# Combining the expert outputs: the first addition of odd tiles as a scaling on ScalarE and an addition on GpSimd

## The reference

```python
gates = g_w * e_w / jnp.sum(e_w, axis=-1, keepdims=True)
yb = lax.map(expert_block, (xb, blk_exp)).reshape(n_slots, d)
y = jax.ops.segment_sum(yb.astype(f32) * slot_gate[:, None], slot_tok, num_segments=n + 1)
# per token: h + g1 * y_rows[slot 1] + g2 * y_rows[slot 2]
out = h * rsqrt(mean(h * h) + NORM_EPS) * norm_final_g
```

## Time and profile before

| | |
|---|---|
| three runs, us | 3441.44, 3448.67 (median), 3459.29 |
| profiled execution, us | 3445.74 |
| its span, first to last instruction, us | 3444.0 |
| busy over the span | PE 92%, DVE 38%, ACT 29%, POOL 10% |
| `combine`, from its first instruction at 3365.75 | some 78 us of the span |

### The profile page before, as it was taken

How to read it: one execution, slowest core, us unless ns; L and a number is a source line. 1 busy time by engine, 2 the same in 40 slices (tenths; PEclk the granted TensorE clock), 3 DMA queues, 4 the chain that set the end, 5 groups by cost and what they waited for, 6 DMA issues and landing times. The chain is left out here.

```text
span 3444.0 us, 75176 instructions
## 1 busy us (share of the span) xinstructions
PE 3163.8 (92%) x31053; PEld 2164.0 (63%) x31054; DVE 1315.9 (38%) x3229; ACT 1014.8 (29%) x2151; POOL 332.8 (10%) x348
## 2 busy tenths in 40 slices
PE   6999999999979988987999979996999999999990
PEld 4677666776758888876877655554555555555550
DVE  3455344553224433434755446664111111111117
ACT  3344433444222222224644453331111111111112
POOL 0000000000010000001433200001101010100104
PEclk9999999999879999998999989997999999999995
DMA  6111111111362342324766555423777786677658
GB/s 209 63 68 66 53 46 63 68 58 45 84 143 105 129 156 107 118 108 141 228 184 177 135 191 184 154 80 135 275 249 274 247 281 216 236 273 249 225 192 306
DMA packets 299222, 544.44 MB, mean 158 GB/s; under 512 B 98338, under 2 KB 122658, under 8 KB 292308
## 3 DMA queue, kind: packets, MB, share of 16 engines
q1 hardware_dynamic: 253052, 401.29, 35.1%
q10 hardware_dynamic: 25128, 66.26, 6.1%
q0 software_dynamic: 20784, 73.15, 5.8%
HBM read 400.66 MB, written 139.98 MB: 157 GB/s over the span
## 5 line engine op out<-in xcount | busy, mean ns | idle before, releaser
L298 PE MATMUL proj_main_ps<-proj_xt,proj_w 128*128 128x257 f32 (+1 forms) x1728 | 390.1, 381 | 0.0
L298 PEld LDWEIGHTS proj_main_ps<-proj_xt,proj_w 128*128 128x128 f32 x1728 | 327.8, 203 | 41.3
L2517 PE MATMUL moe_y_ps<-moe_w,moe_ht 128*64 128x512 f32 x1312 | 302.5, 603 | 3.1 <-ACT moe_ht L2556 3.1
L321 PE MATMUL proj_main_ps<-proj_w,proj_xt 128*128 128x512 f32 (+1 forms) x560 | 248.6, 597 | 0.0
L2265 PE MATMUL out_proj_ps<-out_w,out_ct 128*128 128x512 f32 x544 | 242.3, 599 | 5.7 <-DMA out_w<-in_w_out_dram 5.7
L2567 ACT ACTIVATE moe_sg<-moe_gate 128x256 f32<-128x256 f32 x82 | 31.5, 384 | 535.6 <-PE moe_gate L2501 535.6
L2517 PEld LDWEIGHTS moe_y_ps<-moe_w,moe_ht 128*64 128x64 f32 x1312 | 87.5, 137 | 159.5 <-issue 156.1
L321 PEld LDWEIGHTS proj_main_ps<-proj_w,proj_xt 128*128 128x128 f32 (+1 forms) x560 | 102.9, 185 | 124.4 <-issue 122.8
L1163 DVE COPY_PREDICATED rwkv_t<-ahead_rwkv_cons,rwkv_level_ps 128x512 f32<-128x512 uint32 (+1 forms) x168 | 109.2, 661 | 181.8 <-PE rwkv_level_ps L881 181.6
L2265 PEld LDWEIGHTS out_proj_ps<-out_w,out_ct 128*128 128x128 f32 x544 | 101.8, 192 | 121.9 <-issue 121.9
L2603 DVE COPY moe_y<-moe_y_ps 128x512 f32<-128x512 f32 x82 | 56.7, 692 | 314.9 <-PE moe_y_ps L2517 314.9
(11 more groups left out here) (351 smaller groups left out, 5521.2 us busy)
## 6 DMA issues: line engine op xcount, KB each, us to landing
moe_w<-in_expert_w_dram SPq DMA_DIRECT2D x64, 2048.0 KB, 9.7
y_rows<-rwkv_zero POOLq DMA_DIRECT2D x65, 512.0 KB, 4.8
kept_first_gate<-in_expert_w_dram SPq DMA_DIRECT2D x16, 2048.0 KB, 9.7
kept_first_up<-in_expert_w_dram SPq DMA_DIRECT2D x16, 2048.0 KB, 15.1
y_rows<-moe_y ACTq DMA_DIRECT2D x164, 128.0 KB, 6.1
ft_p<-proj_uf SPq DMA_DIRECT2D x32, 642.0 KB, 3.3
rwkv_feat<-ft_p SPq DMA_DIRECT2D x12, 1284.0 KB, 7.1
att_s_k<-in_cache_att_k_dram ACTq DMA_DIRECT2D x14, 1024.0 KB, 7.3
```

The lines of the kernel that those rows point to most:

```text
L298: last = mm(out[:, 0:w + 1], W[:, k, kind * C + m * P:kind * C + (m + 1) * P], XT[n % 2][:, k, 0:w + 1], start=(k == 0), stop=(k == KT - 1))
L321: last = mm(o, x, W[:, k, j * C:(j + 1) * C], start=(k == 0), stop=(k == KT - 1))
L2517: last = mm(py[j * HB:(j + 1) * HB, :], HT[:, c, r * HB:(r + 1) * HB], W2[s][:, k, j * 512:(j + 1) * 512], start=(k == 0), stop=(k == FE / ...
```

## The change

For odd tiles `add_first` is split in two. ACT multiplies Y1 by the gate in place (`weigh_first`), placed one tile ahead: before its Square of tile t it scales tile t+1 if that is odd. POOL adds the scaled Y1 to HH (`add_weighted`), placed four tiles behind its gathers: before the gathers of tile t it adds tile t-4 if that is odd, and its loop runs four steps further to reach the last ones. DVE's `add_second` of an odd tile waits for POOL's addition; DVE no longer issues `add_first` for odd tiles. Even tiles are computed as before. There are 8 odd tiles (1 to 15).

```diff
+        weighted, added = sem("first_weighted"), sem("weighted_added")
+        apart = lambda t: t % 2 == 1
 ...
         @blk.gpsimd
         def _(g):
-            for t in range(NT):
+            def add_weighted(t):
+                j, R = t % NB, rows(t)
+                g.wait_ge(weighted, t // 2 + 1)
+                nc.gpsimd.tensor_tensor(HH[0:R, t, :], HH[0:R, t, :], Y1[j][0:R], ALU.add).then_inc(added, 1)
+
+            for t in range(NT + 4):
+                if t >= 4 and apart(t - 4):
+                    add_weighted(t - 4)
+                if t >= NT:
+                    continue
                 j, R = t % NB, rows(t)
                 if t >= NB:
                     g.wait_ge(st[j], 16 * (t // NB))
 ...
             def add_second(t):
                 j, R = t % NB, rows(t)
-                v.wait_ge(first, t + 1)
+                if apart(t):
+                    v.wait_ge(added, t // 2 + 1)
+                else:
+                    v.wait_ge(first, t // 2 + 1)
 ...
             for t in range(NT + 1):
-                if t < NT:
+                if t < NT and not apart(t):
                     add_first(t)
 ...
         @blk.scalar
         def _(a):
+            def weigh_first(t):
+                j, R = t % NB, rows(t)
+                a.wait_ge(gat[j], 32 * (t // NB) + 32)
+                nc.scalar.activation(Y1[j][0:R], Y1[j][0:R], ACT.Identity, scale=RG[0:R, t, 0:1]).then_inc(weighted, 1)
+
             for t in range(NT):
                 j, R, n = t % NB, rows(t), N1[t % 2]
+                if t + 1 < NT and apart(t + 1):
+                    weigh_first(t + 1)
                 a.wait_ge(second, t + 1)
```

## The result

The changed kernel takes 3470.51 us (median of nine runs, 3467.45 to 3475.42) against 3442.39 us of the kernel before (nine runs, 3432.79 to 3463.47): 28.1 us more, ratio 1.0076 with a 95% interval of 1.0057 to 1.0096. The prediction said 3476, with 28.8 us of difference. The difference was met within a microsecond; most of the 5.5 us by which the time itself was missed come from the base, since the median of the kernel before is 3442.39 over nine runs, where it was 3448.67 over the first three. The profiled executions have spans of 3472.7 and 3444.0 us.

What follows compares the result with a forecast made beforehand. In `combine`, DVE and the DMA engines were taken as both full; six turns (+23.6), the start (+4.7) and the tail (+0.5) gave +28.8 us, so 3474.5 from the profile, predicted 3476 between two bases, range 3462 to 3490.

Steps and rivals of the forecast that it cites:

- the ring: In `combine`, store(u-1) waits on the add of u, queued behind gathers that wait for store(u-3); 11.9 us per two tiles.
- Store until POOL goes on: In `combine`, from issue of an output store until POOL can issue the gathers waiting for it: 4.2 us.
- Two gather issues: On POOL, two issues of 0.95 us with 0.30 behind each, ahead of the add: 2.5 us.
- Second addition to the end of the normalisation: On DVE, from the start of an odd tile's second addition to the end of the previous tile's normalisation: 2.7 us.
- The turn: Two tiles of `combine`: 4.2 + 2.5 + 2.5 + 2.7 = 11.9 us, where two now take 7.8 (7.97 over tiles 0 to 12).
- The start: Before store 0, the add of tile 1 stands behind ten gather issues on POOL: store 0 moves by +4.7 us.
- The tail: After store 12, the add of tile 15 overlaps the normalisation of tile 13 and may lose up to 1.2; +0.5 us.
- ACT's part: Eight scalings of 128x1024 on ACT, 1.1 us each, covered by its idle time; waiting for the next tile's gathers costs nothing.
- rival A: Not slower: POOL issues gathers in time and the add waits only for ACT's scaling, 7.9 us per two tiles; about 3450; 0.04.
- Rival B: Only shared SBUF reading: each add stops DVE for 2.4 us and saves it 1.2, +9.6 us, 3455; chance 0.06.
- Rival C: DMA engines stay full and the store wait stays 6.1 us: 13.8 a turn, +40.2 us, 3486; chance 0.15.
- Rival D: ACT loads a table for the scaling and again for the root, 2.6 us per odd tile; about +5, 3480; chance 0.05.

Runs made afterwards that it cites:

- the short addition: Changed kernel with POOL's addition covering only the first 64 of 1024 columns of an odd tile, the rest left out: stage 98.9 us, against 106.8 changed and 78.3 before.

## Why the prediction was right

By its terms, with what the trace of the changed kernel has:

- The order on POOL. The add of odd tile u stood behind the gathers of u+3 and the store of u-3, in six turns, as read from the code and the wait of the earlier trace rows. The edits that move the add three tiles behind or take more buffers remove 14.2 and 18.5 us without touching an operation, and the short addition leaves 20.6 us of loss with hardly any arithmetic: that is what shows the ring and rules out the length of the operations as its cause.
- Store until POOL goes on: 4.2 forecast; 4.15 to 4.71 until landing and 0.26 until the issue, so 4.4 to 5.0. Too low by some 0.5. That it came so near is in part luck: its reckoning counted only the gathers right behind the addition, and the run with the short addition, where these stand as before, has a landing of 5.4 to 5.7.
- Two gather issues: 2.5 forecast, 2.2 measured. The 0.30 us behind the second don't arise when an addition follows (3402.09 + 0.93, the addition at 3403.04). The two errors nearly cancel, by luck.
- The addition: 2.4 against 2.35, with handoffs 2.5 against 2.4 (3403.04 to 3405.43). Second addition to the end of the normalisation: 2.7 against 2.7 (3405.43 to 3408.11).
- The turn: 11.9 against 11.9; six of them +23.6 against +23.6.
- The start: +4.7 forecast. Store 0 goes 18.5 us after the gain's load, 14.4 before: +4.1. The 0.30 us behind the last gather issue don't arise here either.
- The tail: +0.5 forecast, +0.8 measured (16.8 us behind store 12 against 16.0), with the 3.41 us operation named in advance as the place of the overlap: 2.1 us lost there less 1.2 us saved is 0.9, within the 1.2 that were named as the most.
- Sum: +28.8 against +28.5 in the profile and +28.1 between the medians.

What was not right: ACT's part was priced at nothing. In the changed kernel that holds, but the run with the addition on DVE shows that it costs some 3.5 us with the ring gone (81.8 against 78.3, one profile of each). DVE's idle time ahead of the odd tiles' second additions was put at 4 to 5 us and is 5.0 to 5.6; the forecast's own terms (a turn of 11.9 less some 6.6 us of DVE's work) give 5.3. And rival A, the side on which the change would not have been slower, was put at 3450 by the scaling's chain; the run with eight buffers shows that POOL's own 8.8 us per two tiles, which I did not reckon, would have stood ahead of it. Rival B named the size of that case (+9.6 against +10.0) by luck: 4.2 of the 10.0 are the later start, and most of the rest is borne by POOL. Rival C (a store wait of 6.1) was the right thing to fear: with the short addition the wait reached 5.9, and 6.8 in the first turn. Rival D fell: the stage has one load of tables, as before.

No version was found that beats the kernel before. The stage with the ring and nearly all of POOL's arithmetic taken away, which doesn't compute the whole result, took 77.5 us against 78.3: a difference too small to be measured in 3442.

## What to carry to other kernels

An engine with idle time isn't an engine that is free at the time needed: look at what it waits for in its own order, and put on it only what may be as late as that wait. If an operation that others need is queued behind gathers that wait for stores of its own results, you get a ring; count its turn term by term, and remember that the transfer in it is no constant: here it grew when the addition ahead of it was shortened. Before taking work off the busiest engine, look for the second full resource: here, with the DMA engines at 1.03 and 420 GB/s, the ring gave back 2.4 of some 7 us of DVE work that it no longer had.

## What the runs showed of the hardware

- DVE operations with two SBUF inputs stand still while POOL adds or copies in SBUF: 128x1024 went from 1.28 us to 3.24 to 3.42 us beside an addition of 2.34 to 2.76, and to 1.86 to 2.53 us beside a one-input copy of 1.04 to 1.35. Each ended 1.07 to 1.09 us behind POOL's operation. Memsets on POOL (0.97 us) held up none.
- It goes the other way too. An indirect gather takes 0.94 us to issue in a quiet stretch; each of the 83 issues of more than 1.15 us began while a DVE operation was under way and ended 0.74 to 0.85 us behind it, after up to 2.00 us. No addition is needed for it: the kernel before has 1.84 us. POOL's addition of 2.35 us took 2.56 to 2.84 us where DVE was at work as it began.
- The landing time of a 512 KB store is a matter of its company: 2.6 us in the quiet tail, 4.2 in the changed kernel (median), 5.8 in the kernel before, up to 8.7 with the add three tiles behind.
- The DMA share near 1 isn't one rate: 0.98 went with 345 GB/s in the changed kernel with eight buffers (3405 to 3423), 1.03 with 420 GB/s in the one with the short addition.
